# Chunk-wise norms in the second mixer of a two-block transformer kernel

## The chip, the cores and the metric

The kernel runs on one core of a Trainium2 chip, as one program. The metric is device time in microseconds. The time before is 2458.33 us, the median of three runs (2453.66 to 2459.83).

## The reference, cut to what matters

Two transformer blocks run one after the other on 256 tokens of width 1024, all in fp32. The first block (a gated attention and recurrence mixer, then a feed-forward layer that gathers rows of a large table) is untouched by the change. The second block is:

```
h     = rms_norm(x, norm1_g) * (1 + sc1) + sh1
z     = h @ w_in                       # u_val, u_gate, q, k, v, f, gate_c, gate_a
conv  = silu(layer_norm(depthwise_conv(u_val * sigmoid(u_gate)))) @ w_conv_out
attn  = forgetting_attention(q, k, v, f) @ w_attn_out
mixed = sigmoid(gate_c) * conv + sigmoid(gate_a) * attn
x     = x + g1 * (mixed @ w_out)
h2    = rms_norm(x, norm2_g) * (1 + sc2) + sh2
x     = x + g2 * moe(h2)               # router, top 4 of 32 experts, 1024 -> 2048 -> 1024
out   = rms_norm(x, final_g)
```

`rms_norm` divides each token by the root of the mean of its 1024 squares.

## The kernel before, in words

Activations lie transposed: `xT` and `hT` are 8 chunks (`KD`) of 128 features by 256 tokens (`T`). Each engine walks the same list of jobs, written out by hand (`plan_second()`), in order: `x2T` 0 to 3, `ss3`, `ug` 0 and 1, `uv` 0 and 1, `f`, `q`, `k`, `v`, then gates and attention heads interleaved, `brc` 0 to 3, `bra` 0 to 3, `wo` 0 to 3, `ss4`, `route` 0 and 1, `x3r`, `g2r`, `h3r`, `rank`, `gT`, `xg`. Most jobs fill one of 8 PSUM banks on TensorE (`B.claim`, then the matmuls, then `full[b]`), and another engine empties it. `mm` is line 745; a 128x256 fp32 matmul stands as two records in the trace. Engines meet only over counting semaphores; `own(...)` issues an instruction and waits for its end. An engine takes its instructions in order, so a wait holds up all that stands behind it.

The first norm of the second mixer goes like this:

- `x2T` i (L940 on TensorE): four transposes bring a pair of chunks into a bank; ScalarE copies the pair into `xT` (L1339). After the fourth copy ScalarE squares all of `xT` at once (L1343) and signals once (`s_sq`).
- `ss3`: TensorE waits for that signal and sums the squares over features with 8 matmuls against ones. ScalarE takes the root into `rstd` (L1346).
- `norm_hB` on VectorE: reciprocal of `rstd` (L1798), 8 instructions that multiply a chunk by its scale column and `rstd` (L1800), a wait for all of them, 8 instructions that add the shift column (L1803), a wait for all of them, then one signal (`s_h`).
- `ug` 0: TensorE waits for that signal, then multiplies the 8 chunks by weights, for two column blocks (`project`, halves 0 and 1).

The second norm is the same chain behind the output projection: VectorE adds each pair of `wo` into `xT` (L1934, `s_x1`), ScalarE squares all of it behind the fourth (L1416), then `ss4`, the root, `norm_hB`, and `route` 0 and 1 on TensorE (8 chunk matmuls of 32 columns each, stationary operand `hT`).

Ahead of `wo`, VectorE merges the two branches pair by pair (L1926, L1928) and signals each pair (`s_mrg`). `wo` 0 waits for all four pairs.

The weights of the second mixer come in by SyncE's queue through a ring of five slots; each slot is loaded anew once its last job has filled its bank. The experts' weights use six slots (2 MB each). The first expert's six are loaded during the second mixer, the last of them behind `wo` 3; from then on SyncE loads a slot for the next expert only when TensorE has finished that job of the present one. The expert loop runs 33 passes of eight jobs.

Of the kernel before, what the change touches and what calls it, by code (L numbers as in the profile page):

```python
# [16 lines left out]
ALU = mybir.AluOpType  # L17
ACT = mybir.ActivationFunctionType
# [6 lines left out]
KD = D // P  # L25
# [274 lines left out]
def build_program(nc, a, out):  # L300
# [6 lines left out]
    with ExitStack() as ctx:  # L307
        def sem(name):
            return ctx.enter_context(nc.semaphore(name))
# [23 lines left out]
        eps = carve("fixed", 2)  # L333
        xT = carve("fixed", KD, T)
        hT = carve("fixed", KD, T)
# [183 lines left out]
        s_sq = sem("squares_ready")  # L519
        s_root = sem("root_ready")  # L520
        s_h = sem("h_ready")
        s_xr = sem("xr_ready")
        s_xc = sem("xc_ready")
        s_ri = sem("rnn_gates_ready")
# [218 lines left out]
        def _(pe):  # L743
            def mm(o, l, r, start, stop):
                return pe.matmul(o, l, r, start=start, stop=stop)  # L745
# [184 lines left out]
            for job in plan_second():  # L930
# [10 lines left out]
                                                x2_rows[:, t, (2 * i + j) * P:(2 * i + j + 1) * P], ident)  # L941
                    last.then_inc(full[b], 1)
                elif kind in ("ss3", "ss4"):
                    pe.wait_ge(s_sq, 6 if kind == "ss3" else 7)
                    B.claim(pe, *job)
                    for c in range(KD):
                        last = mm(ps[:, b, 0:T], ones, xsqB[:, c, :], c == 0, c == KD - 1)
                    last.then_inc(full[b], 1)
                elif kind in ("ug", "uv", "q", "k", "gate"):
                    u = {"ug": 1, "uv": 0, "q": 2, "k": 3, "gate": 5}[kind] + i // 2  # L950
                    w = unit("w_in_2", u).rearrange("p (c n) -> p c n", c=KD)
                    unit_loaded(pe, "w_in_2", u)
                    if kind == "ug" and i == 0:
                        pe.wait_ge(s_h, 2 * KD + 1)
                    B.claim(pe, *job)
                    project(B, job, b, w, 2 * (i % 2), hT, KD, 0)
                    project(B, job, b, w, 2 * (i % 2) + 1, hT, KD, 1).then_inc(full[b], 1)
                elif kind == "v":
                    w = unit("w_in_2", 4).rearrange("p (c n) -> p c n", c=KD)
# [34 lines left out]
                elif kind in ("mean", "var"):  # L994
                    if kind == "mean":
                        pe.wait_ge(s_conv, 1)
                    else:
                        pe.wait_ge(s_csq, 1)
                    B.claim(pe, *job)
                    for c in range(KC):  # L1000
                        last = mm(ps[:, b, 0:T], ones, (conv if kind == "mean" else sqB)[:, c, :], c == 0, c == KC - 1)
                    last.then_inc(full[b], 1)
                elif kind in ("bra", "brc"):
                    name, src = ("w_attn_out_2", attnB) if kind == "bra" else ("w_conv_out_2", conv)
                    unit_loaded(pe, name, 0)
                    if i == 0:
                        if kind == "bra":
                            pe.wait_ge(s_o, HA + HB)
                        else:
                            pe.wait_ge(s_silu2, 1)  # L1010
                    w = unit(name, 0).rearrange("p (c n) -> p c n", c=KC)
                    B.claim(pe, *job)
                    project(B, job, b, w, 2 * i, src, KC, 0)
                    project(B, job, b, w, 2 * i + 1, src, KC, 1).then_inc(full[b], 1)
                elif kind == "wo":
                    if i == 0:
                        pe.wait_ge(s_mrg, 4 + 4)
                    unit_loaded(pe, "w_out_2", i // 2)
                    w = unit("w_out_2", i // 2).rearrange("p (c n) -> p c n", c=KD)
                    B.claim(pe, *job)  # L1020
                    project(B, job, b, w, 2 * (i % 2), mixed, KD, 0)
                    project(B, job, b, w, 2 * (i % 2) + 1, mixed, KD, 1).then_inc(full[b], 1)
                elif kind == "route":
                    if i == 0:
                        pe.wait_ge(s_h, 2 * KD + 2)
                    B.claim(pe, *job)
                    for c in range(KD):
                        last = mm(ps[:, b, 0:E], hT[:, c, i * P:(i + 1) * P], w_r[:, c, :], c == 0, c == KD - 1)
                    last.then_inc(full[b], 1)
                elif kind == "gT":  # L1030
                    pe.wait_ge(s_gr, TT)
                    B.claim(pe, *job)
                    for t in range(TT):
                        last = pe.transpose(ps[0:E, b, t * P:(t + 1) * P], gate_rows[:, t, :], ident)
                    last.then_inc(full[b], 1)
                elif kind == "rank":

                    pe.wait_ge(s_pick, 1)
                    pe.wait_ge(s_poolM, 1)
                    B.claim(pe, *job)  # L1040
                    mm(ps[:, b, 0:E], before, picked[:, 0, :], True, True)
                    mm(ps[:, b, E:2 * E], before, picked[:, 1, :], True, False)
                    mm(ps[:, b, E:2 * E], ones, picked[:, 0, :], False, True)
                    mm(ps[:, b, 2 * E:3 * E], ones, picked[:, 0, :], True, False)
                    mm(ps[:, b, 2 * E:3 * E], ones, picked[:, 1, :], False, True).then_inc(full[b], 1)
                elif kind == "xg":
                    if i == 0:
                        pe.wait_ge(s_sel, 1)
                        pe.wait_ge(s_h3r, 4)
                    B.claim(pe, *job)  # L1050
                    gather(b, i).then_inc(full[b], 1)
                elif kind == "h3r":
                    B.claim(pe, *job)
                    for j in range(4):
                        last = pe.transpose(ps[:, b, j * P:(j + 1) * P],
                                            hT[:, 4 * (i % 2) + j, (i // 2) * P:(i // 2 + 1) * P], ident)
                    last.then_inc(full[b], 1)
                elif kind == "x3r":
                    B.claim(pe, *job)
                    for j in range(4):  # L1060
                        last = pe.transpose(ps[:, b, j * P:(j + 1) * P],  # L1061
                                            xT[:, 4 * (i % 2) + j, (i // 2) * P:(i // 2 + 1) * P], ident)
                    last.then_inc(full[b], 1)
                elif kind == "g2r":
                    if i == 0:
                        pe.wait_ge(s_g2d, 1)
                    B.claim(pe, *job)
                    mm(ps[:, b, :], ones, g2_diag[:, 4 * i:4 * i + 4, :].rearrange("p c j -> p (c j)"),
                       True, True).then_inc(full[b], 1)
                else:  # L1070
                    raise ValueError(job)
# [79 lines left out]
        def _(act):  # L1151
# [180 lines left out]
            for job in plan_second():  # L1332
# [2 lines left out]
                bank = ps[:, b, :]  # L1335
                pair = bank.rearrange("p (a b) -> p a b", b=T)
                if kind == "x2T":
                    B.filled(act, *job)
                    own(act.copy(xT[:, 2 * i:2 * i + 2, :], pair))  # L1339
                    act.sem_inc(free[b], 1)  # L1340
                    act.sem_inc(s_x2, 1)
                    if i == 3:
                        fn(xsqB, xT, ACT.Square).then_inc(s_sq, 1)  # L1343
                elif kind in ("ss3", "ss4"):
                    B.filled(act, *job)
                    own(fn(rstd, ps[:, b, 0:T], ACT.Sqrt, bias=eps[:, 1:2], scale=1.0 / D))  # L1346
                    act.sem_inc(free[b], 1)
                    act.sem_inc(s_root, 1)
                elif kind == "ug":
                    B.filled(act, *job)  # L1350
                    own(fn(sigB[:, 2 * i:2 * i + 2, :], pair, ACT.Sigmoid))
# [52 lines left out]
                elif kind == "var":  # L1404
# [6 lines left out]
                        last = fn(conv[:, c, :], conv[:, c, :], ACT.Silu, bias=col("conv_ln_b", c),  # L1411
                                  scale=col("conv_ln_g", c))
                    last.then_inc(s_silu2, 1)
                elif kind == "wo" and i == 3:
                    act.wait_ge(s_x1, 4 + 4)
                    fn(xsqB, xT, ACT.Square).then_inc(s_sq, 1)  # L1416
                elif kind == "route":
                    act.wait_ge(s_rmax, i + 1)
                    fn(chosen, logits[:, 0:E], ACT.Exp, bias=smallM[:, 0:1]).then_inc(s_rexp, 1)
# [24 lines left out]
            with act.Fori(0, total) as q:  # L1444
# [18 lines left out]
                copy_out("S", selgT, ps[:, EXPERT_BANK["S"], 0:T], s_selgT)  # L1463
                copy_out("D", yg, ps[:, EXPERT_BANK["D"], :], s_yg)
                own.leave_open()
            act.wait_ge(s_y, 1)
            fn(smallM[:, 2:4], smallM[:, 2:4], ACT.Sqrt, bias=eps[:, 1:2], scale=1.0 / D).then_inc(s_yroot, 1)

# [2 lines left out]
        def _(dve):  # L1471
# [322 lines left out]
                    dve.sem_inc(free[4 + 2 * tile + half], 1)  # L1794


            def norm_hB(scale, shift):
                own(dve.reciprocal(rstd, rstd))  # L1798
                for c in range(KD):
                    own.mark(stt(hT[:, c, :], xT[:, c, :], scale[:, c:c + 1], rstd, ALU.mult, ALU.mult))  # L1800
                own.settle()
                for c in range(KD):
                    own.mark(ts(hT[:, c, :], hT[:, c, :], mod[:, shift + c:shift + c + 1], None, ALU.add))  # L1803
                own.settle()
                dve.sem_inc(s_h, 1)

            def select(dst, e, part, gated):

# [24 lines left out]
            for job in plan_second():  # L1833
# [4 lines left out]
                if kind == "ss3":  # L1838
                    dve.wait_ge(s_x2, 4)
                    dve.wait_ge(s_root, 2 + 1)  # L1840
                    norm_hB(scale1, 0)
                elif kind == "ss4":
                    dve.wait_ge(s_root, 2 + 2)
                    norm_hB(scale2, 3 * KD)
                elif kind == "uv":
                    B.filled(dve, *job)
                    dve.wait_ge(s_sig, i + 1)
# [304 lines left out]
```

## Time and profile before

| | |
|---|---|
| median of 3 runs | 2458.33 us |
| lowest and highest | 2453.66, 2459.83 us |
| the profiled execution's own time | 2453.13 us |
| its span, first to last instruction | 2451.4 us |
| mean granted TensorE clock | 0.931 of 2.4 GHz |
| TensorE matmul busy | 2066.6 us (84%) |
| VectorE, ScalarE busy | 983.8 us (40%), 544.5 us (22%) |
| DMA | 784.32 MB, mean 320 GB/s |

Starts in the views are microseconds from the first instruction. A view of instructions gives start, duration of the group, engine, line, operation, what it writes and reads, and in square brackets how long the engine sat idle before it and what ended that. SPq is SyncE's queue. In the view of stages, each engine has its busy time and number of instructions, then come the granted TensorE clock (1.00 is 2.4 GHz, 0.50 is 1.2 GHz), the busy share of the DMA engines and GB/s.

### The profile page before, as it was taken

How to read it: one execution, taken by the hardware profiler on the slowest of the kernel's cores; microseconds unless marked ns; L12 is line 12 of the kernel's file. 1: busy time of each engine (PE TensorE's matmuls, PEld its weight loads, DVE VectorE, ACT ScalarE, POOL GpSimd, SP SyncE). 2: the span in 40 equal slices, each digit the busy share in tenths (PEclk: the TensorE clock that was granted, in tenths of full speed). 3: DMA queues.
4: the chain of work that ended last, by engine and by line, in shares of the span. 5: the costliest groups of instructions: out<-in, count | busy, mean ns of one | idle time of the engine just before them, and what ended most of it. 6: DMA issues, size and time to landing. Idle time of an engine off the chain costs nothing.

```text
span 2451.4 us, 27452 instructions
## 1 busy us (share of the span) xinstructions
PE 2066.6 (84%) x8940; PEld 1172.5 (48%) x8941; DVE 983.8 (40%) x2206; ACT 544.5 (22%) x975; POOL 520.1 (21%) x688
## 2 busy tenths in 40 slices
PE   8998999667657757746799959999999999999997
PEld 7777888323223323322478854444444444444443
DVE  5854556465665675663175241111111111111113
ACT  4626201121021121011114122222222222222221
POOL 0000002566666666666000000000000000000000
PEclk9999999878778878878999979999999999999998
DMA  7352584799999999999443418699999999999995
GB/s 292 138 206 91 236 360 172 282 366 359 363 347 362 360 364 357 360 344 376 189 147 129 155 60 335 259 431 428 428 428 429 429 429 428 428 428 429 429 429 217
DMA packets 111686, 784.32 MB, mean 320 GB/s; under 512 B 13040, under 2 KB 13296, under 8 KB 80144
## 3 DMA queue, kind: packets, MB, share of 16 engines
q1 hardware_dynamic: 37904, 515.18, 50.7%
q0 software_dynamic: 73728, 268.47, 29.6%
q8 instruction: 28, 0.46, 0.1%
q14 instruction: 26, 0.21, 0.0%
HBM read 782.55 MB, written 1.05 MB: 320 GB/s over the span
## 4 chain that ended last, share of the span: by engine, by line
PE 47%; issue 2%; DVE 1%; DMA 1%; ACT 1%; POOL 0%; DVEq 0%; ACTq 0%; POOLq 0%
PE ps L745 42%; PE ps L904 3%; PE ps L1104 1%; DMA ring<-in_peer_v,arena 1%; PE ps L1135 0%; PE ps L1136 0%; PE ps L1061 0%; DVE arena L1800 0%; DVE ring L2051 0%; DVE arena L2053 0%; DVE ring L2052 0%; ACT arena L1339 0%; DVE arena L1803 0%; ACT arena L1411 0%; ACT arena L1416 0%
## 5 line engine op out<-in xcount | busy, mean ns | idle before, releaser
L745 PE MATMUL ps<-ring,arena 128*64 128x512 f32 (+2 forms) x3336 | 748.1, 588 | 44.2 <-issue 40.8
L904 PE MATMUL ps<-ring,arena 128*128 128x512 f32 x1024 | 484.0, 636 | 261.4 <-issue 152.3
L745 PEld LDWEIGHTS ps<-ring,arena 128*64 128x64 f32 (+1 forms) x3336 | 262.7, 140 | 502.5 <-issue 498.2
L745 PE MATMUL ps<-arena,ring 128*128 128x256 f32 x2208 | 487.8, 380 | 13.7 <-issue 8.2
L904 PEld LDWEIGHTS ps<-ring,arena 128*128 128x128 f32 x1024 | 207.7, 205 | 536.5 <-issue 529.2
L745 PEld LDWEIGHTS ps<-arena,ring 128*128 128x128 f32 x2208 | 416.5, 190 | 78.3 <-issue 15.4
L1758 DVE CUSTOM_DVE_ANT_0 ring<-ring,ps 128x1024 f32<-128x1024 f32 x256 | 312.6, 1221 | 268.2 <-DMA ring<-in_peer_u,arena 258.6
L2024 DVE TENSOR_TENSOR arena<-ps,arena 128x512 f32<-128x512 f32 x66 | 45.7, 692 | 652.8 <-PE ps L1104 652.8
L707 POOL DMA_INDIRECT ring<-in_peer_v,arena x256 | 245.3, 958 | 135.3 <-issue 108.2
L1449 ACT COPY arena<-ps 128x512 f32<-128x512 f32 (+1 forms) x198 | 108.4, 548 | 728.2 <-PE ps L745 672.1
L697 POOL DMA_INDIRECT ring<-in_peer_u,arena x256 | 240.9, 941 | 130.2 <-issue 60.8
L745 PE MATMUL ps<-arena 128*128 128x128 f32 (+6 forms) x1486 | 223.5, 306 | 39.6 <-DVEq L2000 13.6
L745 PEld LDWEIGHTS ps<-arena 128*128 128x128 f32 (+2 forms) x1486 | 199.1, 199 | 56.5 <-issue 17.9
L1295 ACT ACTIVATE arena<-arena 128x16 f32<-128x16 f32 x16 | 4.9, 308 | 571.1 <-DVEq L1761 491.4
L689 POOL COPY arena<-arena 128x16 uint32<-128x16 uint32 x16 | 3.2, 203 | 386.8 <-POOLq L688 386.6
L1303 ACT ACTIVATE arena<-arena 128x128 f32<-128x128 f32 x256 | 76.5, 388 | 5.6 <-DVE arena L1765 4.2
L904 PE MATMUL ps<-arena 64*128 64x512 f32 (+2 forms) x312 | 75.2, 579 | 2.6 <-ACTq L1423 1.0
L1519 DVE CUSTOM_DVE_ANT_0 ring<-ring,arena 128x1024 f32<-128x1024 f32 x48 | 56.0, 1222 | 3.2 <-DVE arena L1672 0.7
L1829 DVE SCALAR_TENSOR_TENSOR arena<-arena 128x256 f32<-128x256 f32 x120 | 50.2, 481 | 1.6
L726 POOL MEMSET arena<- 128x128 f32 x1 | 0.2, 205 | 226.5 <-DVEq L1938 226.5
L1816 DVE TENSOR_SCALAR arena<-arena 128x128 f32 (+1 forms) x68 | 16.5, 286 | 76.3 <-issue 70.1
L1449 ACT ACT_TABLE_LOAD x33 | 42.3, 1283 | 16.3 <-ACT arena L1449 15.2
(328 smaller groups left out, 1096.6 us busy)
## 6 DMA issues: line engine op xcount, KB each, us to landing
ring<-in_w_exp SPq DMA_DIRECT2D x192, 2048.0 KB, 17.1
ring<-in_w_in SPq DMA_DIRECT2D x24, 2048.0 KB, 7.9
ring<-in_w_ada SPq DMA_DIRECT2D x12, 2048.0 KB, 8.8
ring<-in_w_out SPq DMA_DIRECT2D x4, 2048.0 KB, 7.8
ring<-in_w_peer_q SPq DMA_DIRECT2D x4, 2048.0 KB, 12.1
ring<-in_w_br_rnn SPq DMA_DIRECT2D x4, 1280.0 KB, 9.3
ring<-in_w_br_attn SPq DMA_DIRECT2D x2, 2048.0 KB, 13.9
ring<-in_peer_u,arena POOLq DMA_INDIRECT x256
```

The costliest lines, as they stand in the source:

```text
L697: pool.indirect_dma_start(out=u_rows[k % 8], out_offset=None, in_=a["peer_u"], in_offset=bass.IndirectOffsetOnAxis(ap=idx_now[:, par, k:k ...
L707: pool.indirect_dma_start(out=v_gath[k], out_offset=None, in_=a["peer_v"], in_offset=bass.IndirectOffsetOnAxis(ap=idx_now[:, par, k:k + 1] ...
L745: return pe.matmul(o, l, r, start=start, stop=stop)
L904: return pe.matmul(o, l, r, start=start, stop=False, skip_group_check=True)
L1104: last = pe.transpose(ps[:, EXPERT_BANK[job], j * P:(j + 1) * P], z_sb[:, n, j * P:(j + 1) * P], ident)
L1303: last = fn(diag[:, par, k, :], ident, ACT.Copy, scale=wts[:, par, k:k + 1])
L1449: own(act.copy(dst, src))
L1519: own.mark(dve.tensor_tensor_reduce(w[:, j, :], w[:, j, :], c_row, 1.0, 0.0, ALU.mult, ALU.add, mod[:, m:m + 1]))
L1758: dve.tensor_tensor_reduce(u_rows[k % 8], u_rows[k % 8], h2_rows[tile], 1.0, 0.0, ALU.mult, ALU.add, dots[:, par, k:k + 1]).then_inc(s_dot, 1)
L1816: own.mark(ts(dst[:, t, :], numbers, slot_of[:, t, at_e], None, ALU.is_equal))
L1829: own.mark(stt(conv[:, c, :], src, w, conv[:, c, :], ALU.mult, ALU.add))
L2024: own(tt(dst.rearrange("p j (h s) -> p j h s", h=2), ps[:, bank, :].rearrange("p (j h s) -> p j h s", j=4, h=2), bias.unsqueeze(3).to_broa ...
```

## The change

Squares are taken per pair of chunks, on ScalarE, right behind the copy of the pair (`x2T`) or the residual add of the pair (`wo`), and `ss3` and `ss4` wait per pair. VectorE only scales the chunks and signals each (`s_scaled`); ScalarE adds the shift of each chunk (an Identity with the shift as bias) and signals each (`s_h`); `ug` 0 and `route` 0 wait chunk by chunk. `wo` 0 waits pair by pair for the merged chunks inside its first half. Three one-column square roots are added on ScalarE: ahead of the first `x2T` copy, at `wo` 0, and behind the expert loop.

```diff
                 elif kind in ("ss3", "ss4"):
-                    pe.wait_ge(s_sq, 6 if kind == "ss3" else 7)
                     B.claim(pe, *job)
                     for c in range(KD):
+                        if c % 2 == 0:
+                            pe.wait_ge(s_sq, (5 if kind == "ss3" else 9) + c // 2 + 1)
                         last = mm(ps[:, b, 0:T], ones, xsqB[:, c, :], c == 0, c == KD - 1)
...
-                    if kind == "ug" and i == 0:
-                        pe.wait_ge(s_h, 2 * KD + 1)
                     B.claim(pe, *job)
-                    project(B, job, b, w, 2 * (i % 2), hT, KD, 0)
+                    project(B, job, b, w, 2 * (i % 2), hT, KD, 0,
+                            (lambda c: pe.wait_ge(s_h, 2 * KD + c + 1)) if job == ("ug", 0) else None)
...
                 elif kind == "wo":
-                    if i == 0:
-                        pe.wait_ge(s_mrg, 4 + 4)
...
-                    project(B, job, b, w, 2 * (i % 2), mixed, KD, 0)
+                    project(B, job, b, w, 2 * (i % 2), mixed, KD, 0,
+                            (lambda c: pe.wait_ge(s_mrg, 4 + c // 2 + 1)) if i == 0 else None)
...
                 elif kind == "route":
-                    if i == 0:
-                        pe.wait_ge(s_h, 2 * KD + 2)
                     B.claim(pe, *job)
                     for c in range(KD):
+                        if i == 0:
+                            pe.wait_ge(s_h, 3 * KD + c + 1)
...
                 if kind == "x2T":
+                    if i == 0:
+                        fn(smallB[:, 23:24], eps[:, 1:2], ACT.Sqrt)
                     B.filled(act, *job)
                     own(act.copy(xT[:, 2 * i:2 * i + 2, :], pair))
                     act.sem_inc(free[b], 1)
                     act.sem_inc(s_x2, 1)
-                    if i == 3:
-                        fn(xsqB, xT, ACT.Square).then_inc(s_sq, 1)
+                    fn(xsqB[:, 2 * i:2 * i + 2, :], xT[:, 2 * i:2 * i + 2, :], ACT.Square).then_inc(s_sq, 1)
                 elif kind in ("ss3", "ss4"):
...
+                    for c in range(KD):
+                        shift = (0 if kind == "ss3" else 3 * KD) + c
+                        act.wait_ge(s_scaled, (0 if kind == "ss3" else KD) + c + 1)
+                        fn(hT[:, c, :], hT[:, c, :], ACT.Identity, bias=mod[:, shift:shift + 1]).then_inc(s_h, 1)
...
-                elif kind == "wo" and i == 3:
-                    act.wait_ge(s_x1, 4 + 4)
-                    fn(xsqB, xT, ACT.Square).then_inc(s_sq, 1)
+                elif kind == "wo":
+                    if i == 0:
+                        fn(smallB[:, 23:24], eps[:, 1:2], ACT.Sqrt)
+                    act.wait_ge(s_x1, 4 + i + 1)
+                    fn(xsqB[:, 2 * i:2 * i + 2, :], xT[:, 2 * i:2 * i + 2, :], ACT.Square).then_inc(s_sq, 1)
...
+            fn(smallM[:, 7:8], eps[:, 1:2], ACT.Sqrt)
             act.wait_ge(s_y, 1)
...
-            def norm_hB(scale, shift):
+            def norm_hB(scale):
                 own(dve.reciprocal(rstd, rstd))
                 for c in range(KD):
-                    own.mark(stt(hT[:, c, :], xT[:, c, :], scale[:, c:c + 1], rstd, ALU.mult, ALU.mult))
-                own.settle()
-                for c in range(KD):
-                    own.mark(ts(hT[:, c, :], hT[:, c, :], mod[:, shift + c:shift + c + 1], None, ALU.add))
-                own.settle()
-                dve.sem_inc(s_h, 1)
+                    stt(hT[:, c, :], xT[:, c, :], scale[:, c:c + 1], rstd, ALU.mult, ALU.mult).then_inc(s_scaled, 1)
```

## Rows read from the trace of the kernel before

**Rows 1.** Stages by time: busy of each engine, clock, DMA share.
```profile
1188.29:1208.70 20.41, 7.38 (x32) 5.83 (x32) 7.20 (x17) 8.37 (x10) 5.28 (x7) 0.84 0.41 143
1208.70:1389.50 180.80, 180.31 (x824) 150.42 (x824) 91.34 (x215) 50.98 (x86) 0.00 (x0) 0.99 0.32 117
1419.20:1474.10 54.90, 29.19 (x136) 24.72 (x136) 27.39 (x73) 13.80 (x19) 5.65 (x9) 0.72 0.14 48
...
1600.00:2433.00 833.00, 792.24 (x4159) 356.46 (x4158) 140.73 (x316) 181.75 (x257) 0.00 (x0) 1.00 0.99 421
```

**Rows 2.** Waits of TensorE between 1188 and 1475 us.
```profile
PE ps L745 <- issue: 8.2, 1, 8.2
PE ps L745 <- DVEq L1805: 8.0, 1, 8.0
PE ps L745 <- ACT arena L1416: 3.1, 1, 3.1
PE ps L745 <- DVEq L1929: 1.7, 1, 1.7
```

**Rows 3.** Timeline of the first norm of the second mixer.
```profile
1188.29 1.07 ACT L1328 COPY arena<-ps 128x512 f32<-128x512 f32 x2 [36.41 <-PE ps L904]
...
1190.12 0.59 ACT L1339 COPY arena<-ps 128x512 f32<-128x512 f32 x1 [0.75 <-PE ps L940]
...
1193.20 1.91 ACT L1343 ACTIVATE arena<-arena 128x2048 f32<-128x2048 f32 x1 [0.18 <-ACT arena L1339]
...
1195.16 5.41 PE L745 MATMUL ps<-arena 128*128 128x256 f32 x16 [3.77 <-ACT arena L1343]
...
1203.10 3.26 DVE L1800 SCALAR_TENSOR_TENSOR arena<-arena 128x256 f32<-128x256 f32 x8
...
1208.74 29.85 PE L745 MATMUL ps<-arena,ring 128*128 128x256 f32 x128 [8.17 <-issue]
...
1242.14 27.99 PE L745 MATMUL ps<-arena,ring 128*128 128x256 f32 x128
```

**Rows 4.** The chain that ended last, behind `wo` 3.
```profile
1419.21 0.89 DVE arena L1934 x2
...
1420.28 1.92 ACT arena L1416
1422.24 3.75 PE ps L745 x16
...
1428.43 3.27 DVE arena L1800 x8
...
1434.02 7.04 PE ps L745 x32
1441.06 3.47 PE ps L1061 x16
```

**Rows 5.** Timeline of ScalarE, VectorE, TensorE at the first block's first norm.
```profile
8.86 1.28 ACT L1158 ACT_TABLE_LOAD   x1
10.15 0.20 ACT L1158 ACTIVATE arena<-arena 128x1 f32<-128x1 f32 x1
...
15.14 3.26 DVE L1527 SCALAR_TENSOR_TENSOR arena<-arena 128x256 f32<-128x256 f32 x8
...
15.77 10.42 PE L745 MATMUL ps<-arena,ring 128*128 128x256 f32 x47 [3.18 <-DVE arena L1527]
```

**Rows 6.** Timeline of ScalarE: two 128x256 instructions with a scale column.
```profile
342.87 0.91 ACT L1272 ACTIVATE arena<-arena 128x256 f32<-128x256 f32 x2 [69.36 <-DVEq L1740]
```

**Rows 7.** Stages of 1 us at which the granted clock changes.
```profile
1205.00:1206.00 1.00, 0.00 (x0) 0.00 (x0) 1.00 (x4) 0.00 (x0) 0.00 (x0) 0.88 0.00 0
...
1444.00:1445.00 1.00, 1.00 (x5) 0.71 (x4) 0.03 (x1) 0.82 (x2) 0.00 (x0) 0.65 0.00 0
```

**Rows 8.** Timeline of SyncE's queue and of ScalarE at the end.
```profile
1481.38 0.87 SPq L633 DMA_DIRECT2D ring<-in_w_exp  x2
...
2434.01 1.28 ACT L1467 ACT_TABLE_LOAD   x1 [0.31 <-ACT arena L1449]
```

More of the change, by code:

```diff
@@ L521, in build_program @@
         s_h = sem("h_ready")
+        s_scaled = sem("scaled_rows_ready")
         s_xr = sem("xr_ready")
@@ L1840, in _ @@
                     dve.wait_ge(s_root, 2 + 1)
-                    norm_hB(scale1, 0)
+                    norm_hB(scale1)
                 elif kind == "ss4":
                     dve.wait_ge(s_root, 2 + 2)
-                    norm_hB(scale2, 3 * KD)
+                    norm_hB(scale2)
                 elif kind == "uv":
```

## The prediction

> **What bounds the kernel now.** I read the stages first. Three limits follow each other. From 1208.7 to 1389.5 us TensorE is busy 180.31 of 180.80 us, so the second mixer is bound by TensorE and whatever starts it earlier ends it earlier. From 1600 to 2433 us the DMA engines are busy 0.99 of the time at 421 GB/s: the expert loop is bound by loading weights. Between these lie two stretches in which neither is full: 1188.29 to 1208.70, with TensorE busy 7.38 of 20.41 us, and 1419.20 to 1474.10, with 29.19 of 54.90 us and a DMA share of 0.14 [rows 1]. All that the change touches stands in or at the edge of these two stretches.
>
> Then the waits of TensorE there: 3.8 us for the full square of `x2T`, 8.2 us for the first norm, 1.7 us for the last merged pair, 3.1 us for the full square behind `wo`, 8.0 us for the second norm [rows 2, 3]. Together they are 24.8 us. The chain that ended last runs through them (its part at the second norm is shown [rows 4]), so here idle time of TensorE is time of the kernel.
>
> **Does a gain here reach the end?** The expert loop is bound by DMA, so this has to be asked. Its loads are not free running: the first load of the loop is issued at 1481.38 [rows 8], when TensorE has finished the first job of expert 0, and each later one hangs on such a release. The six units of expert 0 are issued by `wo` 3 at the latest; between 1419.2 and 1474.1 the DMA engines are at 0.14 [rows 1], so they are idle long before the loop starts. An earlier start of TensorE therefore moves the first release and with it the whole chain of loads, one for one. An absorber would have to be a time that does not move, and the only ones are the end of the row gathering ahead of 1188.29 and the unit loads tied to it, which are used tens of microseconds later.
>
> **Part 1, squares per pair ahead of `ss3`.** ScalarE is free at 1188.29 + 1.07 = 1189.36. The added square root has no wait ahead of it, so its table load goes right there: load and root take 10.15 + 0.20 - 8.86 = 1.49 us in the first block [rows 5], so the first copy starts at about 1190.85 instead of 1190.12 [rows 3]: 0.7 us late. Each pair then takes the copy 0.59, the hand-over to itself 0.18, and a square of 128x512. The full square of 2048 columns takes 1.91 [rows 3] and the two 256-column instructions 0.91 as a pair [rows 6]; between them I take 0.6. That is 1.37 a pair and the last square ends at 1190.85 + 4 x 1.37 = 1196.3, 1.2 us later than now (1195.11). But TensorE then has 4 of the 16 records left instead of all. At full clock 16 take 3.75 [rows 4], so 4 take 0.94 and with the pipe's depth about 1.2; at 1.2 GHz about 2.0. `ss3` ends at 1197.5 to 1198.3 instead of 1195.16 + 5.41 = 1200.57. Gain 2.3 to 3.1, I take 2.9.
>
> The Trainium skill (ScalarE: Activation LUTs, What ACT_TABLE_LOAD costs) puts a switch of tables at 1.28 us and a further 1.38 us of draining. The row does not agree: the load starts 0.01 us behind the square before it and the root follows 0.01 us behind the load [rows 5]. By the page the sum would be 1.4 us smaller; it goes by the row.
>
> **Part 2, the first norm by chunks.** Now TensorE starts 1208.74 - 1203.10 = 5.64 us behind the first scaling [rows 3]. The first block has a norm that signals chunks straight from VectorE to TensorE: there TensorE starts 15.77 - 15.14 = 0.63 us behind the first scaling and is not held up afterwards [rows 5]. The new chain has one instruction more between them, an Identity on ScalarE with one column as operand. The nearest row is the copy with a scale column: two in 0.91, so about 0.50 for one and 0.41 for each that follows [rows 6]. With one more hand-over, about as long as that from VectorE to TensorE (0.63 less one scaling of some 0.5, so 0.12), I get 0.63 + 0.50 + 0.12 = 1.25 us. VectorE's scalings come every 3.26 / 8 = 0.41 us [rows 3], TensorE needs 3.75 / 8 = 0.47 a chunk at most [rows 4], ScalarE 0.41: nobody falls behind if ScalarE overlaps them; if the wait ahead of each stops that, it is 0.50 a chunk and 0.6 us more over eight. Gain 5.64 - 1.25 = 4.4, at least 3.8. Behind the Identities ScalarE has only the table load for the sigmoid of `ug` 0, whose bank needs another 3.7 us of TensorE, so that is hidden; without that cover it would cost 1.28.
>
> The same page (Rules for kernel authors) says to do an add on VectorE and not on ScalarE. The rows agree on the single instruction (0.50 us against (1434.02 - 1428.43 - 3.27) / 8 = 0.29 on VectorE [rows 4, 6]). Kept on VectorE between the scalings, a chunk would take 0.41 + 0.29 = 0.70 us, and as eight of them take 5.6, 2.3 more than now set the pace, part 2 would gain about 2 instead of 4.4; as the two engines work side by side here, I follow the rows.
>
> **The clock, first norm.** Now TensorE idles 8.17 us [rows 3], its clock falls to half at 1205.9 [rows 7], 5.3 us behind the end of `ss3`, and the first matmuls of `ug` run at 1.2 GHz: the first 128 records take 29.85 us, the same count from 1242.14 on takes 27.99 [rows 3]. So 1.9 us are lost to the clock, which means that it was back after some 3.8 us of matmuls. Afterwards the idle time is 2.5 (root and reciprocal, as now) + 1.25 = 3.8 us. In the first block 3.18 us of idle time at the same place left the clock alone [rows 5]. I expect the clock to hold mostly and take 1.2 of the 1.9; bounds 0 and 1.9.
>
> **Part 3, merged chunks in order.** `wo` 0 starts 1.7 us late now [rows 2]. Three of four pairs are merged by then, and 6 chunks of the first half are 2.6 us of work, more than the 1.7 us that the last pair still needs. The stall goes whole: 1.7. The weights of `wo` lie in the ring already.
>
> **Part 4, squares per pair ahead of `ss4`.** The first three pairs are squared behind `wo` 1, 2 and 3, on an idle ScalarE. TensorE goes from `wo` 3 into 6 chunks of `ss4` without a stop (to 1419.2 + 2.8 = 1422.0), while VectorE's last add ends at 1420.1 and a square from 1420.28 ends at 1420.9 [rows 4]: 1.1 us in time. The wait of 3.1 us [rows 2] goes, and a little of refilling the pipe: 3.3. The added root at `wo` 0 is hidden in ScalarE's idle time; the load it moves was hidden too, so it is worth nothing.
>
> **Part 5, the second norm by chunks.** Now `route` 0 ends half of 7.04 us behind 1434.02, at 1437.6, 9.1 us behind the first scaling at 1428.43 [rows 4]. Afterwards: 1.25 to the start, 7 chunks at 0.41, one chunk of 0.44: 4.6 us. Gain 4.5 (3.9 if the Identities come every 0.50). What follows, `route` 1 and the transposes, keeps its order and, at the half clock that it has now, its length. ScalarE loads the exponential's table behind the last Identity, 1.28 us; VectorE asks for the exponential only behind `route` 0's end and some small instructions of its own, when the load should be done; if not, it is late by a fraction of those 1.28. The clock: it now stays at half until 1444.6 [rows 7]. It may stay up this time, since the idle time is shorter; then `route` 1 and the transposes, 3.5 us each now [rows 4], take half, a gain of up to 3.4. Against this, `route` 0 fed at 0.41 us a chunk gives TensorE little to do. I take 0; it may also rise later than now, which I price at -1.5.
>
> **Part 6, the end.** The table load for the last norm already sits right behind the last copy, at 2434.01, where TensorE and VectorE have 10 us to go [rows 8]. The added root changes nothing: 0.
>
> **The sum.** 2.9 + 4.4 + 1.2 + 1.7 + 3.3 + 4.5 = 18.0 us. The profiled execution's own time is 2453.13 (span 2451.4), which would become 2435.1. It lies 5.2 us under the median of the runs; from the median, 2458.33 - 18.0 = 2440.3 us.
>
> **Rivals.**
> - *Clock stays up at the router too*: gain 18 + 3.4 = 21.4, 2436.9 us. For it: less idle time. Against: the router's matmuls of 32 columns did not bring the clock up in 7 us [rows 4, 7]. Chance 0.15.
> - *Hand-overs cost more and the clock falls anyway*: 2.3 + 3.8 + 0 + 1.6 + 3.2 + 3.9 - 1.5 = 13.3, 2445.0 us. For it: a new relay of three engines per chunk that no row shows as a whole. Chance 0.17.
> - *The gain is absorbed* by something that does not move, ahead of or in the expert loop: 2458 us. It would need a load that is late now; the waits of TensorE in this stretch name none [rows 2]. Chance 0.03.
> - *Slower*: the clock. Fed in small portions, TensorE could drop to 1.2 GHz at `ss3` and stay there through `ug`, `uv` and `f`. At half clock each microsecond of work takes two. To end slower by 0.3% it must eat 18 + 7.4 = 25.4 us, so 51 us at half clock, nearly all of `ug` and `uv` (29.85 us now [rows 3]); with both whole, and so nothing of the 1.2 for the clock, it would be 2458.3 - 16.8 + 28 = 2469.5 us. Against it: now, after a longer idle time, the clock was back within 3.8 us of dense work. Chance 0.01.
>
> The forecast itself has 0.64. A measurement of this kernel can tell about 0.3%, 7.4 us, from no change; all cases but the last two lie beyond it, and I add a little for the noise between runs: faster 0.94, same 0.04, slower 0.02.
>
> **The range.** Gains from 13.3 to 21.4 (22.1 with the whole 1.9 of the first clock) give 2436.2 to 2445.0 from the median; the runs before lie from 4.7 under it to 1.5 above. With that, 2432 to 2447.
>
> **What will show it.** Right: TensorE's waits at L1343 and L1416 gone or under 1 us; `ug` starting some 1.25 us behind the first scaling; no wait ahead of `wo` 0; `ss4` starting with `wo` 3's end; the expert loop's first load near 1463 us and the same distance from there to the end. Wrong: Identities more than 0.5 us apart; the clock at 0.50 in `ug`; the first copy of `x2T` later than 1191.5; a longer expert loop.

## The result, and the profile after

The changed kernel takes 2440.51 us, the median of five runs (2435.36 to 2442.65), against 2459.64 for the kernel before (five runs, 2453.66 to 2462.07). The ratio is 0.993, with a 95% interval of 0.9912 to 0.9948 (the two medians alone give 0.992). The forecast was 2440.3. Executions that ran over 1.5% above the fastest of the same kernel, in a slower state of the chip, are left out of every median here and below.

The profiled execution spans 2439.8 us, 11.6 less than before. One view tells where. From the copy behind the last gathered row (L1328) to the first load of the expert loop the kernel before takes 1481.38 - 1188.29 = 293.09 us; call this the stretch. The timeline after, ScalarE's copy and SyncE's load:

```profile
1193.73 1.07 ACT L1328 COPY arena<-ps 128x512 f32<-128x512 f32 x2 [38.56 <-PE ps L905]
...
1469.71 7.71 SPq L634 DMA_DIRECT2D ring<-in_w_exp  x4
```

The stretch is now 275.98 us, 17.11 shorter. From that load to the end it is 2451.4 - 1481.38 = 970.0 before and 2439.8 - 1469.71 = 970.1 after: the expert loop passes the gain on whole. The rest, 5.4 us the other way, is the start of the copy (1188.29, now 1193.73). It lies ahead of all that the change touches, and moves from run to run: in the profiles taken for this study it lies between 1187.65 and 1194.21. So the stretch is the measure of what follows. It leaves out that part of the scatter; most of what is left comes from TensorE's clock, and the experiments show how much that can be.

TensorE's waits in the stretch after, longest first (engine and line that waited, what ended it, total, times, longest):

```profile
PE ps L746 <- DVEq L2003: 13.6, 1, 13.6
PE ps L746 <- ACT arena L1353: 8.2, 2, 4.5
...
PE ps L746 <- ACT arena L1344: 1.2, 3, 0.9
```

The longest is TensorE waiting for VectorE's ranks, 13.6 us before as well. L1353 is the new Identity, L1344 the square per pair. Of the waits before [rows 2, 3] the square behind `wo` (3.1) and the merged pairs (1.7) are gone, the square ahead of `ss3` is 1.2 instead of 3.8, and the two norms are 8.2 together instead of 16.2. The first norm after, to be read beside [rows 3]:

```profile
1194.82 1.28 ACT L1339 ACT_TABLE_LOAD   x1
...
1196.23 0.57 ACT L1341 COPY arena<-ps 128x512 f32<-128x512 f32 x1
...
1200.86 0.63 ACT L1344 ACTIVATE arena<-arena 128x512 f32<-128x512 f32 x1 [0.18 <-ACT arena L1341]
1201.54 1.13 PE L746 MATMUL ps<-arena 128*128 128x256 f32 x4 [0.16 <-ACT arena L1344]
1202.71 0.47 ACT L1347 ACTIVATE arena<-ps,arena 128x256 f32<-128x256 f32 x1 [1.23 <-PE ps L746]
...
1205.20 3.26 DVE L1808 SCALAR_TENSOR_TENSOR arena<-arena 128x256 f32<-128x256 f32 x8
1205.72 3.30 ACT L1353 ACTIVATE arena<-arena 128x256 f32<-128x256 f32 x8 [2.53 <-DVE arena L1808]
1206.37 29.64 PE L746 MATMUL ps<-arena,ring 128*128 128x256 f32 x128 [3.70 <-ACT arena L1353]
```

Eight Identities take 3.30 us, as long as the eight scalings beside them: the relay loses nothing. TensorE starts 1206.37 - 1205.20 = 1.17 us behind the first scaling, instead of 5.64. The second norm looks different, in the same columns:

```profile
1420.13 1.49 POOL L739 CAST arena<-arena 128x1568 f32<-128x1568 int32 x1
1420.56 4.11 DVE L1808 SCALAR_TENSOR_TENSOR arena<-arena 128x256 f32<-128x256 f32 x8
1421.94 3.30 ACT L1353 ACTIVATE arena<-arena 128x256 f32<-128x256 f32 x8 [3.31 <-DVE arena L1808]
1422.59 7.01 PE L746 MATMUL ps<-arena 128*128 128x32 f32 x32 [4.48 <-ACT arena L1353]
```

The same eight scalings take 4.11 us, and ScalarE starts 1.38 us behind the first of them instead of 0.52. The view of that line says why: its instructions last 472 ns at the least, 480 in the middle, and 1340 at the most. One of them was held up while GpSimd's cast ran, from 1420.13 to 1421.62.

### The profile page after: what moved, and what is told of

Same layout as the page of the kernel before. It is cut to its first block, busy times and chain, and to the rows that moved or that the text cites. A ratio compares the mean times of both kernels' runs of the same rounds, so it can differ in the third digit from the quotient of the medians.

```text
span 2439.8 us, 27459 instructions
## 1 busy us (share of the span) xinstructions
PE 2067.6 (85%) x8940; PEld 1173.3 (48%) x8941; DVE 981.6 (40%) x2190; ACT 552.4 (23%) x1000; POOL 519.0 (21%) x688
## 3 DMA queue, kind: packets, MB, share of 16 engines
HBM read 782.55 MB, written 1.05 MB: 321 GB/s over the span
## 4 chain that ended last, share of the span: by engine, by line
PE 47%; issue 2%; DVE 1%; DMA 1%; ACT 1%; DVEq 0%; POOL 0%; ACTq 0%; POOLq 0%
PE ps L746 42%; PE ps L905 3%; PE ps L1104 1%; DMA ring<-in_peer_v,arena 1%; PE ps L1135 0%; PE ps L1136 0%; DVE arena L1806 0%; PE ps L1061 0%; DVE ring L2054 0%; ACT arena L1344 0%; DVE arena L2056 0%; DVE ring L2055 0%; ACT arena L1416 0%; ACT arena L1341 0%; DVE arena L1808 0%
## 5 line engine op out<-in xcount | busy, mean ns | idle before, releaser
L746 PEld LDWEIGHTS ps<-arena,ring 128*128 128x128 f32 x2208 | 419.3, 191 | 75.3 <-issue 13.6
L746 PE MATMUL ps<-arena 128*128 128x128 f32 (+6 forms) x1486 | 222.6, 306 | 28.2 <-DVEq L2003 13.6
## 6 DMA issues: line engine op xcount, KB each, us to landing
ring<-in_w_exp SPq DMA_DIRECT2D x192, 2048.0 KB, 17.1
```

## Experiments

Each was compared by its stretch, in one profiled execution of each kernel, and each diff is against the changed kernel. Line numbers move by a few from kernel to kernel.

**The first norm alone, twice.** Of the change only the parts around `x2T`, `ss3` and `ug` are made; `wo` 0, `ss4` and `route` wait as before.

```diff
+                    if kind == "ss4":
+                        pe.wait_ge(s_sq, 10)
                     for c in range(KD):
-                        if c % 2 == 0:
-                            pe.wait_ge(s_sq, (5 if kind == "ss3" else 9) + c // 2 + 1)
+                        if kind == "ss3" and c % 2 == 0:
+                            pe.wait_ge(s_sq, 5 + c // 2 + 1)
...
-                    norm_hB(scale2)
+                    norm_whole(scale2, 3 * KD)
```

> Only the first norm (squares per pair behind x2T, shifts on ScalarE, ug 0 by chunks) is changed; wo and the second norm are as before. Measured from the copy behind the last gather (L1328) to the first load of the expert loop, the kernel before takes 293.1 us, the changed one 276.0. Theory (the gains add and pass through the TensorE-bound mixer): 8.0 us less than before, 285.1. Rival (part of the gain of 17.1 appears only when both norms are changed): 287 or more. From that load to the end 970.0 in either case; if the expert loop took back a part, it would be longer by it.

Measured: stretch 288.71, the rest 969.65, time 2448.34. That is 4.4 less than before, not 8.0, and looks like the rival. But where the second norm's root starts, the loss is already there, and one row of the timeline holds it:

```profile
1414.27 6.54 PE L746 MATMUL ps<-arena 128*128 128x256 f32 x16 [3.16 <-ACT arena L1425]
```

`ss4` took 6.54 us where it took 3.75 before [rows 4], behind the same idle time of 3.1 us. The granted clock fell to 1.2 GHz within that idle time, at 1413.2, 2.1 us behind the end of `wo` 3 (the 2.7 us in the expectation below is misread). So the same kernel was run again.

> The kernel with only the first norm changed, once more. In its first profile the clock fell 2.7 us behind wo 3, inside the 3.1 us wait for the full square, and ss4 took 6.5 us instead of 3.7. Theory (whether the clock falls there is chance, and without that the gains add): if ss4 takes 3.7 this time the stretch is 285 to 286; if it takes 6.5 again, 288.7. Rival (the gains don't add): 288.7 with ss4 at 3.7.

```profile
1417.64 3.71 PE L746 MATMUL ps<-arena 128*128 128x256 f32 x16 [3.16 <-ACT arena L1425]
```

Measured: `ss4` 3.71, stretch 284.67, the rest 969.26. The gain is 8.4, so nothing of the first norm's gain depends on the second. Of the 4 us between two runs of one kernel 2.8 are the clock in `ss4`; the rest lies behind it, mostly in the row jobs and in `xg`. The pair-wise squares behind `wo` may thus do more than was counted for them: they leave no idle time ahead of `ss4`, and in none of the profiles with them did the clock fall there.

**The second norm alone.** The mirror image: `ss4`, the shifts of the second norm and `route` as in the change, all else as before.

```diff
-                    norm_hB(scale1)
+                    norm_whole(scale1, 0)
...
+                    if i == 0:
+                        pe.wait_ge(s_mrg, 4 + 4)
                     unit_loaded(pe, "w_out_2", i // 2)
```

> Only the second norm (squares per pair behind wo, shifts on ScalarE, route 0 by chunks) is changed; first norm and wo 0 as before. Same measure. Theory: 3.3 for the squares and 3.6 for the norm, 6.9 less, 286.2, give or take 1 for the clock in the transposes and token gathers behind it. Rival: as above, 288 or more. The first scaling of the second norm should again take 1.34 us instead of 0.48, beside GpSimd's 1568-column cast.

Measured: stretch 285.80, 7.3 less than before; the scalings take 4.11 us again. With the first norm's 8.4 (293.09 - 284.67) this makes 15.7, so the gains of the two norms add. The 1.4 that are left of 17.1 are `wo` 0 (1.7 of wait in both kernels here, none in the changed one), within the scatter of the clock.

**GpSimd's constants later.**

```diff
             pool.wait_ge(s_x1, 4 + 4)
+            pool.wait_ge(s_h, 4 * KD)
             own.mark(pool.memset(before, 1.0))
```

> The changed kernel, but GpSimd makes its expert constants only when all shifts of the second norm are done. Theory (GpSimd's last cast, 1.49 us, held up VectorE's first scaling): that scaling takes 0.48 us instead of 1.34, ScalarE's first Identity starts 0.52 us behind it instead of 1.38, and the stretch is 275.1 instead of 276.0. Rival (the first scaling is slow by itself, or waits for a reader of hT): still 1.34 and 276.0.

```profile
1416.34 3.26 DVE L1809 SCALAR_TENSOR_TENSOR arena<-arena 128x256 f32<-128x256 f32 x8
...
1416.86 3.30 ACT L1354 ACTIVATE arena<-arena 128x256 f32<-128x256 f32 x8 [2.46 <-DVE arena L1809]
...
1424.64 1.50 POOL L740 CAST arena<-arena 128x1568 f32<-128x1568 int32 x1
```

The scalings take 3.26, ScalarE follows after 0.52, and TensorE waits 3.62 us for it instead of 4.48: the 0.86 us are back and the cause is shown. The stretch nevertheless came out at 277.07, not 275.1. `ug`'s first 128 records took 30.95 us here (29.64 in the changed kernel) and the gather of tokens `xg` 6.69 (5.33): 2.7 us of clock, in places that the edit does not touch. The row jobs behind the router took 0.6 us less, which makes up the difference.

**Shifts on VectorE.** ScalarE has no Identities; VectorE scales chunk c, then shifts chunk c - 1 and signals it.

```diff
+                for c in range(KD + 1):
+                    if c < KD:
+                        stt(hT[:, c, :], xT[:, c, :], scale[:, c:c + 1], rstd, ALU.mult, ALU.mult).then_inc(s_scaled, 1)
+                    if c > 0:
+                        dve.wait_ge(s_scaled, n + c)
+                        ts(hT[:, c - 1, :], hT[:, c - 1, :], mod[:, shift + c - 1:shift + c], None,
+                           ALU.add).then_inc(s_h, 1)
```

> The changed kernel, but VectorE adds the shifts itself, each one behind the next chunk's scaling, and signals each chunk; ScalarE has no Identities. Theory (the relay over ScalarE is what gives the second half of the gain): 0.41 + 0.27 = 0.68 us a chunk; ug 0 some 1 us later, route 0 ends 7 x 0.27 = 1.9 and 0.2 us later, the stretch 279 instead of 276.0. Rival (adds belong on VectorE, and the signal per chunk alone gives the gain): 276 or less.

Measured: stretch 278.27. The scalings come 0.66 us apart, `ug` 0 starts 0.1 us later than in the changed kernel, and `route` 0 and 1 take 8.34 us instead of 7.01. So a signal per chunk on one engine gives most of the gain. Of the 2.3 us between the two kernels 1.45 lie between the root of the second norm and the router's result, where the slower pace shows. Another 1.05 are `ug`'s first 128 records (30.69 us instead of 29.64); these took 29.48 to 31.01 us in kernels whose first norm ends in the same Identities, so this part is not shown to come from the pace. TensorE was at 1.2 GHz in `ug`'s first chunks, where it needs about 0.8 us a chunk itself (8 such matmuls in 6.54 us in `ss4` above), more than the 0.66. For this chain the rule to keep adds on VectorE (the Trainium skill, ScalarE: Activation LUTs, Rules for kernel authors) does not hold: following it costs at least the 1.45 us.

**Without the added square roots.** First without the one ahead of `x2T` (the first two lines), then without all three.

```diff
-                    if i == 0:
-                        fn(smallB[:, 23:24], eps[:, 1:2], ACT.Sqrt)
...
-                    if i == 0:
-                        fn(smallB[:, 23:24], eps[:, 1:2], ACT.Sqrt)
...
-            fn(smallM[:, 7:8], eps[:, 1:2], ACT.Sqrt)
```

> The changed kernel without the square root ahead of the first x2T copy. Theory (a table load costs its 1.28 us and hides behind ss3's matmuls): first copy 0.67 us earlier, the load starts with the last square's end and is done when ss3 is, ss3's root 0.5 to 0.7 us earlier relative to the last gather. Rival (a switch of tables costs 2.66 us, as the Trainium skill, ScalarE: Activation LUTs, What ACT_TABLE_LOAD costs, puts it): root about 0.8 us later than in the changed kernel.

> The changed kernel without the three added square roots. Theory (a load of 1.28 us sits in idle time of ScalarE except behind ss3's last square, where it costs what the late first copy costs): ss3's root within 0.2 us of the changed kernel's relative to the last gather, ss4's root not later (load right behind the last square at 0.63 + 1.28 = 1.91 us, ss4's matmuls end 1.8 us behind it), the end the same. Rival (the roots are needed): 1.3 us later at ss4 and at the end.

The second of these, ScalarE around `ss3`:

```profile
1198.92 0.63 ACT L1342 ACTIVATE arena<-arena 128x512 f32<-128x512 f32 x1 [0.18 <-ACT arena L1339]
1199.56 1.28 ACT L1345 ACT_TABLE_LOAD   x1
1200.86 0.47 ACT L1345 ACTIVATE arena<-ps,arena 128x256 f32<-128x256 f32 x1
```

The load starts 0.01 us behind the square and the root 0.02 us behind the load: 1.28 us and no more. The root comes 1200.86 - 1192.44 = 8.42 us behind the copy of the rows; in the changed kernel it is 8.98. Without the first root alone it was 8.89, not the 0.5 to 0.7 us less that were expected: there the transposes ahead ran at 1.2 GHz (3.68 us instead of 1.97), and the first copy came 0.2 us earlier instead of 0.67. At `ss4` and at the end nothing moves. The stretch is 277.33 and 274.95. The first added root costs 0.6 us, the other two are worth nothing.

**TensorE kept busy in its gaps.** Filler matmuls against ones, into a bank that the next job overwrites: eight ahead of `ug` 0 and eight ahead of `route` 0.

```diff
+            def keep_busy(b, n):
+                for _ in range(n):
+                    mm(ps[:, b, 0:T], ones, xT[:, 0, :], True, True)
...
+                    if job == ("ug", 0):
+                        keep_busy(b, 8)
...
+                    if i == 0:
+                        keep_busy(b, 8)
```

> The changed kernel with 8 filler matmuls of 256 columns (3.5 us at full clock, results overwritten) ahead of ug 0 and as many ahead of route 0, where TensorE idles 3.7 and 4.5 us. Theory (the idle time costs the clock, and the clock costs time): clock 1.00 in both places, the first 128 records of ug 28.0 us instead of 29.6, route 0 and 1 about 5 us instead of 7.0, the ten transpose and row jobs behind them 2.6 us shorter; the stretch 270 instead of 276. Rival (the router's narrow matmuls lower the clock whatever stands ahead of them): only ug gains, 1.6 to 2.5 us, 274.

Measured: stretch 273.79. `ug`'s 128 records take 27.99 us, the steady figure of [rows 3], so the first half of the theory holds. At the router the rival is right: the clock fell to 0.50 at 1419.8, with TensorE busy, in the middle of the 32-column matmuls, which took 6.44 us instead of 7.01. (In the changed kernel it falls at 1421.5, already in the idle time ahead of them.)

The next kernel adds the late constants and fills a third gap, the 13.6 us in which TensorE waits for VectorE's ranks (`keep_busy(b, 30)` ahead of `xg`, 13 us of filler); the one after it also a small matmul between the router's chunks:

```diff
                         if i == 0:
+                            if c > 0:
+                                mm(ps[:, B.bank("x3r", 0), 0:P], ones, xT[:, 0, 0:P], True, True)
+                            else:
+                                B.claim(pe, "x3r", 0)
                             pe.wait_ge(s_h, 3 * KD + c + 1)
```

> The changed kernel with GpSimd's constants late and with filler matmuls in three gaps: 8 ahead of ug 0, 8 ahead of route 0, 30 (13 us) ahead of the token gather xg behind the 13.6 us of VectorE's rank chain. Theory: 1.6 (ug) + 0.9 (GpSimd) + 0.5 (start of route) + 1.8 (xg: 32 matmuls in 3.5 us instead of 5.3 to 6.7) less: 271. Rival (filler falls short in the long gap too, the clock falls within it): xg as before, 273.

> The kernel of the three gaps with one more filler matmul of 128 columns between the chunks of route 0 (0.22 us at full clock, inside the 0.41 us a chunk that ScalarE sets). Theory (the router's 32-column matmuls give too little work to hold the clock): clock stays at 1.00 through route 0 and 1 and x3r, route 1 1.8 us instead of 3.5, x3r 1.9 instead of 3.65: 3 us less than with three gaps. Rival (the clock falls in route 1 or the filler delays route 0 as much): 0 to 1 less.

Measured: stretch 270.32 and 267.40. `xg` takes 3.84 us with the third gap filled, and with the filler in the router the rows below follow one another at full clock (TensorE's timeline of the last kernel, taken in the timed run below):

```profile
1420.48 5.29 PE L747 MATMUL ps<-arena 128*128 128x32 f32 x46 [0.17 <-ACT arena L1368]
1425.61 1.95 PE L1076 MATMUL ps<-arena 128*128 128x128 f32 x16
...
1432.12 13.11 PE L747 MATMUL ps<-arena 128*128 128x256 f32 x60
1445.88 3.84 PE L747 MATMUL ps<-arena 128*128 128x128 f32 x32 [0.64 <-DVEq L2018]
```

The router's 46 records (14 of them filler) take 5.29 us where 32 took 7.01, the 16 transposes behind them 1.95 instead of 3.65 in the changed kernel. The filler is not free: the router's first result comes 0.4 us later than with three gaps alone. But the row jobs behind it take 3.3 us less. GpSimd's late cast, too, has only been moved: it now runs beside VectorE's small router instructions, and one that takes two inputs from SBUF (128x32) lasts 0.90 us instead of 0.19. Here it costs nothing: VectorE waits for TensorE's row jobs behind it.

**The last kernel and the changed one, timed on one chip.**

> The changed kernel once more, as a yardstick on the chip of the next one: ratio 0.993, stretch from the last gather to the expert loop 275 to 278, depending on the clock at ug, the row jobs and xg.

> The kernel with GpSimd's constants late, filler in three gaps and between the chunks of route 0, timed. Theory: 8.6 us under the changed kernel (276.0 - 267.4), ratio to before about 0.9895, and the stretch the same again within 0.3 us, because TensorE's clock no longer falls in it by chance. Rival (the one profile was lucky): stretch scatters by 1 to 3 us as in the others.

Measured: the changed kernel 2438.20 us, ratio 0.9927 (0.9914 to 0.9940), stretch 275.64. The last kernel 2433.08, ratio 0.9901 (0.9884 to 0.9917), its slowest run (2435.14) under the fastest of the changed one (2435.35). Its stretch is 267.40 again, to the hundredth, where the two kernels with idle gaps that were profiled twice differ by 0.3 us (the changed one) and 4.0 us (the first norm alone). Between the medians lie 5.1 us, not the 8.6 that were expected, nor the 8.2 between the stretches. That the rest is scatter of the part ahead is likely, since that part alone moves by 6.6 us between profiles, but not shown.

## Why the prediction was right

Each term of its sum, and what the two profiles show for it:

- *Squares per pair ahead of `ss3`*, 2.9 forecast. `ss3` ends 8.94 us behind the row copies instead of 12.28: 3.3. The copies start 0.67 late as worked out, the pairs come 1.29 apart and not 1.37, since a copy overlaps the square ahead of it.
- *First norm by chunks*, 4.4: 5.64 - 1.17 = 4.5.
- *The clock at `ug`*, 1.2: 29.85 - 29.64 = 0.2. This term was mis-sized. The idle time went from 8.2 to 3.7 us, and I took the first block's 3.2 us without a fall as a sign that it would hold. It fell nevertheless, at 1206.5, 3.8 us behind the end of `ss3` and just as `ug`'s first matmul ran; before it fell 5.2 us behind (the prediction reads 5.3). The filler kernel shows what was at stake, 29.64 - 27.99 = 1.65, and the repeated runs show that no single profile of the kernel before could have told: the same 3.1 us behind `wo` 3 left the clock alone in one run and cost 2.8 us in another.
- *Merged chunks in order*, 1.7: from the last merge to `wo` 3's add it is 27.72 us (1414.68 - 1386.96) instead of 29.67: 1.95. The wait went whole, and so did the refilling of the pipe.
- *Squares per pair ahead of `ss4`*, 3.3: from that add to the root 3.47 instead of 6.80, 3.3.
- *Second norm by chunks*, 4.5: from the root to VectorE's first router instruction 8.08 instead of 11.68, 3.6. The step that failed is the assumption that the chain would run as it does in the first norm. Everything on the way there had become 3.3 us faster, except GpSimd, which starts its constants at the same signal as before (`wo` 3's add). Before, its last cast ended 2.3 us ahead of the first scaling; now they overlap and VectorE loses 0.86 us. The same is shown the other way round by GpSimd's later start.
- *The end*, 0: the added root runs at 2423.74, 8.6 us ahead of its use. Right.
- Not in the sum: the row jobs behind the router are 0.95 us longer, since the clock rises later, and `xg` is 1.16 shorter, since it rises earlier. Together 0.2.

3.3 + 4.5 + 0.2 + 1.95 + 3.3 + 3.6 + 0.2 = 17.1, the whole difference of the stretches, against 18.0. The two misses of about 1 us pointed the same way, and part of them was made good by small gains. That the medians differ by 19.1 and hit the forecast so closely is partly luck, given an interval of some 9 us.

The argument about passing the gain on was right, and is the one that mattered: 970 us from the first load to the end in the kernel before and the changed one, and 968.5 to 970.1 in all others. Of the rivals, the one with costlier hand-overs fell (Identities 0.41 us apart), though its other half, a clock that falls anyway at `ug` and rises later at the router, came true. The one with a clock that stays up at the router fell too: in the changed kernel the clock fell in the idle time ahead of `route` 0, and the reason given against this rival, the narrow matmuls, holds as well, since with that time filled it fell among them. The slower one had a true core, the clock, but it would have had to take 25.4 us, where the late rise behind the router cost 0.95.

## What to carry to other kernels

Where one engine is the limit before a gap and another behind it, price the gap by its waits and ask whether what follows starts from a signal or from a time; here it was a signal, and each microsecond came through. When a chain is shortened, look at what starts from the same signal on the engines beside it: it has not moved, and may now lie across the chain. Idle time of TensorE costs more than itself where the clock falls in it, and no single profile tells whether it will; here filler took that cost away, and two profiles of the filled kernel agree to the hundredth.

## What the runs showed of the hardware

- A 128x256 scaling on VectorE with two inputs in SBUF took 1.34 us instead of 0.48 beside a GpSimd cast from SBUF to SBUF, and ended 0.3 us behind it; a reciprocal with one input took its 1.75 us both beside two smaller GpSimd jobs, an iota and a 128x512 cast, and alone. The Trainium skill (SBUF — State Buffer, Who interferes with whom) says that these two engines share a pair of ports under an exclusive lock, and that a VectorE instruction with two SBUF inputs contends with a GpSimd instruction that reads SBUF. The rows agree.
- The granted clock can fall from 2.4 to 1.2 GHz with TensorE busy: in the router's matmuls of 32 columns, 3.3 us behind their start, with 3.5 us of dense filler ahead of them. With a 128-column matmul between the chunks of `route` 0 it stayed at 2.4 GHz, in both profiles.
- It fell 2.1 us behind the last matmul in one run and not within 3.1 us in another run of the same kernel.
